# Turning rows into features by DMA instead of on TensorE, in a fused encoder step on 8 cores

## What is computed

```
z = x @ w_in                       # [u | v | B | C | x_in], 5 x 512 columns
v = layernorm(v per head); a = u * (w_s @ v, per block of 128 rows)
b = B * causal_conv3(C * x_in)
x = layernorm(ALPHA * x + [a, b] @ w_out)            # mixer
p = softmax(q(x) . mem_k / 16)
x = layernorm(ALPHA * x + (p @ mem_v) @ w_mem_o)     # memory cross-attention
f = (silu(x @ w_gate) * (x @ w_up)) @ w_down         # 2816 wide
y = layernorm(ALPHA * x + f)
```

## Time and profile before

| | |
|---|---|
| median of 3 runs | 3460.51 us (3454.98 to 3743.6) |
| the profiled execution's own time | 3471.73 us |
| its span on the slowest core (core 2) | 3470.2 us; the eight cores 3429.2 to 3470.2 us |
| PE (TensorE matmul) busy | 3272.9 us, 94% |
| DVE busy | 1949.7 us, 56% |
| ACT busy | 899.7 us, 26% |
| POOL busy | 333.0 us, 10% |
| chain that ended last | PE 76%, DMA 8%, DVE 7% |
| moved by DMA | 601.52 MB, mean 173 GB/s |

### The profile page before, as it was taken

The page is one execution under the profiler, slowest core; times in us unless marked ns, Lnnn a source line. Parts: engine busy times, 40 slices in busy tenths (PEclk is TensorE's granted clock), DMA queues, the critical chain, the costliest instruction groups (busy, mean ns, idle before and its releaser), DMA issues.

```text
span 3470.2 us, 49386 instructions; the slowest of 8 cores (3429.2 to 3470.2 us)
## 1 busy us (share of the span) xinstructions
PE 3272.9 (94%) x16482; PEld 1538.2 (44%) x16808; DVE 1949.7 (56%) x3428; ACT 899.7 (26%) x1687; POOL 333.0 (10%) x355
## 2 busy tenths in 40 slices
PE   5787999997999999999999999999999999999998
PEld 2433444443444444445344444444444444444443
DVE  4454554654656567565465656656564755656553
ACT  1421323222232231322223223231322223132320
POOL 1111101110001010010000101000010101000000
PEclk8789999998999999999999999999999999999997
DMA  9799899469474535445345453545445453544442
GB/s 165 134 218 199 169 233 219 165 193 213 174 184 173 192 122 208 153 178 199 109 169 186 152 197 138 204 147 207 151 152 205 141 215 138 194 163 164 183 146 79
DMA packets 95751, 601.52 MB, mean 173 GB/s; under 512 B 10992, under 2 KB 13168, under 8 KB 35408
## 3 DMA queue, kind: packets, MB, share of 16 engines
q1 hardware_dynamic: 82272, 507.17, 40.3%
q0 software_dynamic: 11808, 87.17, 15.7%
q10 hardware_dynamic: 1424, 4.02, 0.5%
HBM read 620.58 MB, written 71.18 MB: 199 GB/s over the span
## 4 chain that ended last, share of the span: by engine, by line
PE 76%; DMA 8%; DVE 7%; issue 4%; ACT 4%; another core or an unknown queue 1%; POOL 0%; DVEq 0%; SPq 0%; ACTq 0%; POOLq 0%
PE bank L332 74%; DMA ringA<-wpk 2%; DVE st L567 2%; PE bank L530 2%; DVE mv L569 1%; DMA ringB<-wsc 1%; ACT F L583 1%; ACT Pf L690 1%; DMA xbuf<-x_prompt 1%; DMA wsc<-ringA 1%; DMA fsc<-xbuf 1%; DMA wsc<-ringB 1%; DVE xbuf L803 1%; DVE nmx L687 1%
## 5 line engine op out<-in xcount | busy, mean ns | idle before, releaser
L332 PE MATMUL bank<-feat,ringB 128*128 128x512 bf16 x5516 | 1255.7, 382 | 14.3 <-DMA ringB<-wpk 4.9
L332 PEld LDWEIGHTS bank<-feat,ringB 128*128 128x128 bf16 x5632 | 552.6, 98 | 681.3 <-issue 47.1
L332 PE MATMUL bank<-ringB,hT 128*128 128x512 bf16 x2627 | 609.9, 382 | 33.4 <-DMA ringB<-wpk 23.8
L778 DVE TENSOR_TENSOR hT<-bank,scr 128x512 bf16<-128x512 f32 x352 | 238.2, 690 | 506.0 <-PE bank L332 291.1
L332 PE MATMUL bank<-ringA,F 128*128 128x512 bf16 x1927 | 449.5, 384 | 24.2 <-DMA ringA<-wpk 16.0
L332 PE MATMUL bank<-feat,ringA 128*128 128x512 bf16 x1995 | 457.2, 383 | 4.3 <-DMA ringA<-wpk 1.7
L500 POOL TENSOR_TENSOR rs<-ve,mhalf 128x1 f32<-128x1 f32 (+1 forms) x195 | 219.7, 1127 | 2463.2 <-DVE ve L498 2443.4
L332 PEld LDWEIGHTS bank<-ringB,hT 128*128 128x128 bf16 x2696 | 260.3, 98 | 341.1 <-issue 50.6
L523 ACT ACTIVATE row<-xbuf 128x1024 bf16<-128x1024 f32 x128 | 135.3, 1057 | 1043.4 <-DVE xbuf L513 1043.4
L332 PE MATMUL bank<-ringA,feat 128*128 128x512 bf16 x1449 | 336.2, 383 | 41.1 <-DMA ringA<-wpk 16.8
L332 PEld LDWEIGHTS bank<-feat,ringA 128*128 128x128 bf16 x2048 | 198.9, 99 | 234.2 <-issue 18.8
(11 more groups left out here) (118 smaller groups left out, 1852.5 us busy)
## 6 DMA issues: line engine op xcount, KB each, us to landing
ringB<-wsc SPq DMA_DIRECT2D x205, 1024.0 KB, 6.3
ringA<-wsc SPq DMA_DIRECT2D x103, 1024.0 KB, 6.9
ringA<-fsc SPq DMA_DIRECT2D x62, 1024.0 KB, 10.7
ringB<-wpk POOLq DMA_DIRECT2D x34, 1024.0 KB, 15.7
xbuf<-x_prompt SPq DMA_DIRECT2D x64, 512.0 KB, 8.9
y_prompt<-xbuf SPq DMA_DIRECT2D x64, 512.0 KB, 2.9
ringA<-wpk POOLq DMA_DIRECT2D x22, 1024.0 KB, 19.3
ringB<-wsc SPq DMA_DIRECT2D x25, 768.0 KB, 5.8
```

The lines of the kernel that those rows point to most:

```text
L332: op("tensor", lambda e: e.matmul(out, lhsT=lhsT, rhs=rhs, start=start, stop=stop), reads=reads, writes=writes)
L778: op("vector", lambda e: e.tensor_tensor(out=hT[:, f, :], in0=bu, in1=sg[:, 0:512], op=ALU.mult), reads=[bbu, bsg], writes=[b_hT[f]])
```

## The change

From `t` = 5 on (`TDMA = 5`, the sixth tile) the rows of all four subs are turned by a DMA with `transpose=True`, issued from ACT's queue straight after the row is written, from the row buffer to the same place in `feat` or `F1`. For these tiles TensorE's transposes and ACT's copies out of PSUM are gone, and `x_to_feat` does nothing. The sample rows keep the old way. Four shifts come with it:

- the mixer's rows are cast (`x_row`) after the two gate/up units that follow the projection and not before them, in all tiles from 1 on;
- when the tile before was turned by DMA (`late`), the four v units stand together, and the gate/up unit that stood between the second and the third is written after the fourth, with the next one;
- in the score stage of such tiles (but those of the sample rows) the pair for `scores` alternates between banks 4-5 and 6-7 (`pairs` (4, 6)); it was 4-5 alone;
- in the memory stage the second down half's 22 steps stand 3, 3, 3, 13 behind the four projections; they stood 5, 6, 5, 6.

```diff
+TDMA = 5
...
+            s.dma = t >= TDMA
...
+        def x_row(s):
             SP = s.SP
             s.row, s.brow = take_row()
             op("scalar", lambda e, r=s.row: e.activation(out=r[0:SP, :], in_=s.x[0:SP], func=AF.Copy), reads=[s.bx], writes=[s.brow])
+            if s.dma:
+                turn_dma(s, s.F0, [s.bF0], "tx%d" % s.j)
...
+        def turn_dma(s, dst, b_dst, stream):
+            op("scalar", lambda e, r=s.row: e.dma_start(out=dst, in_=r[0:s.SP, :], transpose=True), reads=[s.brow], writes=b_dst, dma=stream)
+
         def x_to_feat(s):
+            if s.dma:
+                return
             to_feat(s.row, s.brow, s.SP, s.F0, [s.bF0])
...
         def p_to_feat(s):
+            if s.dma:
+                turn_dma(s, s.F1, s.bF1, "tp%d" % s.j)
+                return
             to_feat(s.row, s.brow, s.SP, s.F1, s.bF1)
...
             v_norm(subs[0])
-            f(1, True)
+            late = prev[0].dma
+            if not late:
+                f(1, True)
             in_v(subs[2], pc)
...
             v_norm(subs[2])
-            f(1, True)
+            f(1 + late, True)
             v_norm(subs[3])
...
             for j in range(4):
-                proj_resid(subs[j], pc, subs[j].F1, subs[j].bF1, 0)
+                proj_resid(subs[j], pc, subs[j].F1, subs[j].bF1, 0, False)
                 f(2)
+                x_row(subs[j])
                 if j:
                     x_to_feat(subs[j - 1])
...
-            zone[0], pairs[0] = (6,) if smp_f else (6, 7), (4,)
+            zone[0], pairs[0] = ((6,) if smp_f else (6, 7), (4,)) if smp_f or smp or not subs[0].dma else (range(4, 8), (4, 6))
...
             d = down_half(prev, 1)
-            d(5)
+            share = (3, 3, 3, 13) if subs[0].dma else (5, 6, 5, 6)
+            d(share[0])
...
-            d(6)
+            d(share[1])
             x_to_feat(subs[0])
             proj_resid(subs[2], pc, subs[2].F1, subs[2].bF1, 1)
-            d(5)
+            d(share[2])
...
-            d(6)
+            d(share[3])
```

More of the change, by code:

```diff
@@ L363, in sample_sub @@
             s.sample = True
+            s.dma = False
             return s
@@ L515, in ln_shift, with ln_full @@
                reads=[s.bx, bR, buf("lnb%d" % li)], writes=[s.bx])
-        def ln_full(s, li):
+        def ln_full(s, li, now):
             ln_rstd(s, li)
@@ L520, in ln_full @@
             ln_shift(s, li)
+            if now:
+                x_row(s)
+        def x_row(s):
             SP = s.SP
@@ L534, in to_feat, with proj_resid @@
             give(bb)
+        def turn_dma(s, dst, b_dst, stream):
+            op("scalar", lambda e, r=s.row: e.dma_start(out=dst, in_=r[0:s.SP, :], transpose=True), reads=[s.brow], writes=b_dst, dma=stream)
         def x_to_feat(s):
+            if s.dma:
+                return
             to_feat(s.row, s.brow, s.SP, s.F0, [s.bF0])
-        def proj_resid(s, pcs, src, b_src, li):
+        def proj_resid(s, pcs, src, b_src, li, now=True):
             SP = s.SP
@@ L550, in proj_resid @@
                 give(bb)
-            ln_full(s, li)
+            ln_full(s, li, now)
         def in_v(s, pc):
```

## The result

| | before | after |
|---|---|---|
| median | 3454.98 us (3453.85 to 3460.51, 3 executions) | 3486.56 us (3477.08 to 3491.73, 4 executions) |
| ratio after / before | | 1.0084, 95% interval 1.0051 to 1.0117 |
| the eight cores, profiled execution | 3429.2 to 3470.2 us, median 3448.3 | 3394.9 to 3490.2 us, median 3442.3 |

The forecast was 3405 us, 1.6% faster, with a range of 3378 to 3475 us; the change made the kernel 0.8% slower. Executions in which one half of the chip ran at a lower clock are left out of all ratios and medians here, one of 3743.6 us of the kernel before among them (the 3460.51 us ahead of the prediction counts it), and one experiment, e9, has no ratio for that reason.

A forecast was written before the change was run, and what follows sets the result against it. TensorE was taken as the bound in every late tile. Gains of 58.1 (transposes) and 16.7 us (score waits), less 16.6 (fourth softmax rows) and 3 (last turn), gave 55 us: 3460.5 to 3405 us, range 3378 to 3475.

The forecast's parts named there:

- What bounds the kernel: TensorE is the bound in every late tile; whatever leaves its stream comes out of the time.
- transposes removed: 12 sets of eight transposes leave TensorE in each of 11 tiles, 0.44 us each: 58.1 us gained.
- v units together: Wait for v's norm ahead of `wT`: at best 0.6 us less in 10 tiles, at worst doubled; taken as 0.
- a microsecond or two either way: Expected change in the tiles with sample rows.
- Waits in the score stage: Two pairs of banks remove waits of 1.12 and 0.73 us in nine tiles: 16.7 us gained.
- (a): Fourth sub's softmax rows, before the fourth memory output: 7.1 us against 5.55 of cover, 1.5 us wait in 11 tiles, -16.6 us.
- (b): Fourth sub's last rows, before the first gate/up unit: 7.6 us of cover against 6.7, so no wait.
- The last turn's wait: Gate/up units wait 6.1 us for the last rows' DMA, there being no v units; -3 us with the clock.
- (c): The other six DMAs of the softmax and last norm, and the mixer's four, have 13 us or more of cover.
- I charge the ring loads nothing: Turning DMAs add 3.1 MB a tile, 9 us of full DMA; no cost to the weight loads was counted.
- rival 3: Turning DMAs run one behind the other on ACT's queue, 20.9 us against (a)'s 5.55: +117 us, 3577 us; chance 0.13.
- The clock: Matmuls after a long TensorE wait run slower: 1.4 us for each longer wait, charged in the last turn.

The follow-up runs named there:

- e9: Changed kernel with the fourth sub's mixer rows alone turned on TensorE again; 3481.84 and 3496.47 us.
- e1: Changed kernel in which the load of the next tile's rows waits until the fourth mixer DMA has landed; 3443.3 us, ratio 0.9941.
- e10: Changed kernel without the loads of input rows for tiles 6 to 15, the mixer reusing an earlier tile's rows; 3421.8 us, ratio 0.9891.
- e7: Changed kernel with all four shifts but no turning DMA, every row turned on TensorE; 3456.0 us, ratio 0.9976.
- e6: Changed kernel with the fourth sub's mixer and last rows on TensorE and old shares 5, 6, 5, 6 in the sample turn; 3424.51 us, ratio 0.9858.
- e4: Kernel before with only the alternating score pairs added, from tile 5 on except in the sample turns; 3450.7 us, ratio 0.9967.
- e8: e6 with the load of the next tile's rows also waiting for the third sub's mixer DMA; 3425.55 and 3427.21 us, ratio 0.9904.

## Why the prediction was wrong, step by step

**What bounds the kernel; transposes removed; v units together** held. The shortest tiles are 191.7 us after and 191.0 in e1 and e10, against 191.95 forecast. A set of transposes is worth (197.9 - 192.6 - 0.2) / 10 = 0.5 us (e7 against e6, ten sets, less a wait of 0.2 us for ACT's copy), near the 0.44 of the sum. The wait for v's norm did not grow but went, 0.4 to 0.9 us in each tile from the ninth on, which the forecast had as its best case and took at nothing. In turn 6 the shifts cost 6 us, where "a microsecond or two either way" was allowed. (Between the last output projection and the first gate/up unit of the kernel before stood two sets of transposes, as its listing shows, and not three.)

**Waits in the score stage**: gone in after, as said. The prediction put it down to the pairs alone, and that was half the reason: without the DMAs 0.73 of the 1.85 us stay (e4).

**(a)** was sized too high. It was to wait 1.5 us in each of 11 tiles, 16.6 us. After has 16 such waits in 88 stages, 0.39 us in the median, 0.9 us a core. From the end of the first sub's cast to the landing of the second of the two DMAs it took 4.65 us in the median where 7.1 was taken; that DMA lands in 3.2 us and not in 6.4. The cover was 5.4 us, as counted (5.55). Some 16 us that were charged here were never paid; they hid a part of the errors below, which is luck.

**(b)** failed: "(b) waits nothing". The cover was right (7.5 us in the median for 7.6), but the DMA took 8.7 us from the end of the cast to its landing, and not 6.7. The issue of 1.25 us, for which 0.33 was copied from a plain DMA, lies within that. So 57 of the 80 turns before the last wait, 2.35 us in the median and 25.9 us a core. In some turns it is more: in turn 12 of e10 all eight cores waited 5.1 to 8.8 us, with no load of rows about; there the DMA landed in 14.5 us (core 0) beside a `ringB` load that took 15.3. Why that turn was not found. The last turn's wait was forecast as 6.1 us and is 6.92 in the median.

**(c) and "I charge the ring loads nothing"** are the step that broke the forecast for the slowest core. Twelve DMAs were counted by their bytes, 9 us of full DMA a tile; the share rose by (0.67 - 0.48) x 194.8 = 37 us, for 12672 packets. Of that some 29 us are the turning DMAs' own (14.8% on their queue), the rest is that other packets took longer beside them. And one landing time, 6.4 us, was used for all twelve, wherever they stand. The four mixer DMAs were said to have 13 us or more; but the fourth takes 21 us in the median beside the weight loads and the casting load of rows (e10: 15.8 without that load), the softmax DMAs issued behind it up to 37, and the score unit and the memory outputs wait, 25.4 us a core. With that load gone the slowest core of e10 is at 3433.7 us where after has 3490.2. This is near to rival 3's "fill the DMA queues and starve the rings", but at another place than (a) and in some tiles of some cores only. And the rings did not starve: TensorE waited 1.1 us for a ring load on the slowest core; what came late were the turned rows.

**The clock** was charged once, 1.4 us in the last turn. After the wait of 0.54 us above, 16 matmuls took 3.61 us, full pace; after the first row below, 24 matmuls took 6.92 us instead of 5.34, and a stretch across them shows a clock of 0.57:

```profile
2545.40 6.92 PE L333 MATMUL bank<-feat,ringB 128*128 128x512 bf16 x24 [2.26 <-DMA feat<-row]
```

```profile
2545.00:2549.00 4.00, 3.60 (x10) 1.37 (x11) 2.46 (x12) 2.43 (x7) 0.60 (x2) 0.57 0.01 4
```

Behind the 66 waits for rows of over 2 us on the eight cores the next 24 matmuls took longer than due, by 1.8 us in the median and 15.4 us a core together. That this is the clock was read in a few stretches only.

**The account.** A core was to gain 55 us; in the mean of the eight profiled cores it gained 4 (3450.75 to 3446.5). Better than forecast were (a), by 15.7 us, and v's norm, by 5.4. Worse were (b) by 25.9, the other memory outputs by 19.1, the score unit by 6.3, the clock by 15.4 - 1.4 = 14.0, turn 6 by 6 and the last turn's wait by 0.8. That makes 51 us for the 51 that are missing; so close an agreement is partly chance, since the terms are good to some microseconds. For the slowest core the rows waits are 94 us, 35 more than the mean, and the loss behind them 24 us, 9 more: 3446.5 + 35 + 9 = 3490.5, against 3490.2.

**A mean, where the metric is a maximum.** The sum was made for one core. A cost that falls at random on tiles and cores comes into the time with its worst core: 41 us of spread became 95. No rival had that.

The Trainium skill was quoted with two rules. The first is that turning DMAs are as fast as plain ones ("Advanced Engine Details and Errata", section X-Bar Transpose (TRN2)). With nothing beside it one landed in 3.1 us, like the plain one of the earlier trace rows. In engine time they are not: in the good stretch above 0.87 MB turned took a share of 0.283 and 4.43 MB of SP's DMAs one of 0.491, 2.9 times as much for each byte. The second is that a 128x128 block takes 1309 ns by DMA ("VectorE: DVE Perf Modes", section The three transpose paths). Eight blocks landed in 3.1 us, so it does not add up over blocks; but the page's advice to use TensorE where PSUM will do was right here for the fourth sub's mixer and last rows.

## What to carry to other kernels

Before work is moved from a full engine to the DMA engines, sort the DMAs by place and ask for each what is in flight beside it and what stands behind its issue on the same engine; count packets and their time, not bytes. Turn by DMA where the neighbours are few. Leave on TensorE the rows whose DMA stands beside a cluster of loads, or whose cover is no longer than a landing at that place (here 7.5 us against 8.7): two sets of twelve went back for 1.6 us a tile and removed 57 us of waits a core. And read the spread of the cores with the span: a change can improve the middle core and lose by the slowest.

## What the runs showed of the hardware

- A turning DMA of 128x1024 two-byte elements held ACT's sequencer for 1.25 us in the median and up to 27 us when the DMA engines were behind; a plain one 0.36. It landed in 3.1 us alone, in the median in 8 beside two or three loads of 1 MB, in 14 to 16 beside four, and in 21 (at most 47) with a casting load of rows among them.
- Its packets of 250 bytes held a DMA engine for 36 ns each in the mean in a good stretch and 143 ns in the jam, where 1 MB loads took 28 us. For each byte that is 2.9 times the engine time of SP's DMAs, most of them weight loads, in the good stretch.
- A jam can start from turning DMAs and weight loads alone (turn 8 of e8 and e1: 22.2 to 42.7 us for a turning DMA); with a casting load from POOL's queue beside them it was far more frequent (after against e1 and e10).
- TensorE lost 6.92 - 5.34 = 1.6 us in the 24 matmuls behind a wait of 2.26 us, at a granted clock of 0.57 in 4 us across it, and 5.22 - 3.62 = 1.6 us in the 16 matmuls behind one of 15.47 us. Behind one of 0.54 us it lost nothing.
